# Two-layer decoder trunk on one core: the opening's loads, splits, squares and angle tables rearranged

## The reference, cut to what matters

```python
def rms_norm(x, g):
    xf = x.astype(jnp.float32)
    y = xf * lax.rsqrt(jnp.mean(xf * xf, axis=-1, keepdims=True) + RMS_EPS)
    return (y * g.astype(jnp.float32)).astype(x.dtype)

def rope_tables(positions, dim):
    inv_freq = ROPE_THETA ** (-jnp.arange(0, dim, 2, dtype=jnp.float32) / dim)
    ang = positions.astype(jnp.float32)[..., None] * inv_freq
    return jnp.cos(ang), jnp.sin(ang)

z = rms_norm(x, norm_g) @ w_in          # x: 1024 positions x 1024 channels
```

## Time and profile before

| | us |
|---|---|
| median of 3 runs | 2283.16 |
| the runs | 2282.97 to 2283.17 |
| the profiled execution's own time | 2282.51 |
| its span in the profile | 2280.4 |
| TensorE busy in the span | 2262.1 |
| start of the sum over `ssum` on TensorE | 31.23 |

### The profile page before, as it was taken

The page is one execution under the profiler, slowest core; times in us unless marked ns, Lnnn a source line. Parts: engine busy times, 40 slices in busy tenths (PEclk is TensorE's granted clock), DMA queues, the critical chain, the costliest instruction groups (busy, mean ns, idle before and its releaser), DMA issues.

```text
span 2280.4 us, 27214 instructions
## 1 busy us (share of the span) xinstructions
PE 2262.1 (99%) x10747; PEld 1869.2 (82%) x10747; DVE 1198.3 (53%) x1175; ACT 572.2 (25%) x888; POOL 881.8 (39%) x395
## 2 busy tenths in 40 slices
PE   9999999999999999999999999999999999999999
PEld 7677778888888888888888898888888888888887
DVE  7766774454555555455644244443545555554553
ACT  6455442211111111111343433422111111111110
POOL 1222217534443444334543333275334433443341
PEclk9999999999999999999999999999999999999999
DMA  5111112111111111111321021031111111111111
GB/s 196 54 47 47 33 66 80 46 50 47 46 50 52 46 46 46 55 46 51 111 84 56 27 67 63 14 138 46 56 47 46 46 55 46 46 46 54 47 47 74
DMA packets 38577, 132.29 MB, mean 58 GB/s; under 512 B 4896, under 2 KB 6752, under 8 KB 38496
## 3 DMA queue, kind: packets, MB, share of 16 engines
q1 hardware_dynamic: 35760, 122.24, 16.9%
q10 hardware_dynamic: 2736, 8.91, 1.0%
HBM read 118.26 MB, written 8.68 MB: 56 GB/s over the span
## 4 chain that ended last, share of the span: by engine, by line
PE 94%; DVE 4%; ACT 1%; issue 1%; DMA 0%; SPq 0%; DVEq 0%; ACTq 0%
PE pj L1362 42%; PE dn L1382 17%; PE pj L347 14%; PE pj L325 5%; PE pj L1826 3%; PE dn L1430 3%; PE dn L686 1%; PE pj L710 1%; PE pj L1430 1%; PE pj L506 1%; PE pj L696 1%; PE dn L1964 1%; PE dn L1973 1%; PE dn L1852 1%; PE pj L1852 1%
## 5 line engine op out<-in xcount | busy, mean ns | idle before, releaser
L1627 POOL TENSOR_TENSOR w_hi<-w_raw,ones 128x1024 fp32r<-128x1024 f32 x186 | 355.8, 1913 | 1336.9 <-PE pj L1362 564.0
L1629 POOL TENSOR_TENSOR w_lo<-w_raw,w_hi 128x1024 fp32r<-128x1024 f32 x186 | 468.2, 2517 | 14.5
L1471 DVE SCALAR_TENSOR_TENSOR ffn_y<-ffn_h,params,ffn_y 128x1024 f32<-128x1024 f32 x176 | 323.5, 1838 | 117.6 <-ACT ffn_y L1479 109.1
L1479 ACT ACTIVATE ffn_y<-ffn_h,params 128x1024 f32<-128x1024 f32 x88 | 109.6, 1245 | 886.6 <-DVE ffn_h L1460 886.6
L1460 DVE TENSOR_TENSOR ffn_h<-pj,rms_bc 128x1024 f32<-128x1024 f32 x88 | 107.8, 1224 | 365.6 <-PE pj L1362 351.9
L1520 DVE TENSOR_TENSOR res<-dn,res 128x1024 f32<-128x1024 f32 x144 | 176.1, 1223 | 115.4 <-PE dn L1382 115.4
L1362 PE MATMUL pj<-xb_hi,w_hi 128*128 128x512 f32 x704 | 216.9, 389 | 0.0
L1362 PE MATMUL pj<-xa_hi,w_hi 128*128 128x512 f32 x704 | 216.9, 389 | 0.0
L1362 PE MATMUL pj<-xb_lo,w_hi 128*128 128x512 f32 x704 | 216.7, 389 | 0.0
L1362 PE MATMUL pj<-xa_hi,w_lo 128*128 128x512 f32 x704 | 216.7, 389 | 0.0
L1362 PE MATMUL pj<-xa_lo,w_hi 128*128 128x512 f32 x704 | 216.7, 389 | 0.0
(11 more groups left out here) (314 smaller groups left out, 3555.0 us busy)
## 6 DMA issues: line engine op xcount, KB each, us to landing
w_raw<-weights SPq DMA_DIRECT2D x189, 512.0 KB, 3.5
x_first<-x_t SPq DMA_DIRECT2D x8, 512.0 KB, 8.7
res<-x_t SPq DMA_DIRECT2D x8, 512.0 KB, 7.4
scratch<-res ACTq DMA_DIRECT2D x8, 512.0 KB, 2.6
res<-scratch SPq DMA_DIRECT2D x8, 512.0 KB, 7.3
y_t<-res ACTq DMA_DIRECT2D x8, 512.0 KB, 2.6
q_turned<-q_raw SPq DMA_DIRECT2D x16, 128.0 KB, 2.3
k_turned<-k_raw SPq DMA_DIRECT2D x16, 128.0 KB, 2.3
```

The costliest lines, as they stand in the source:

```text
L1471: dve.scalar_tensor_tensor(y[:, :], h[:, SH - lag:SH - lag + S], f.tap(j, m, q), y[:, :], ALU.mult, ALU.add).then_inc(taps[f.l], 1)
L1479: act.activation(f.y[m][:, :], f.h[m][:, SH:SH + S], ACT.Identity, bias=f.tap(j, m, 3), scale=f.tap(j, m, 2)).then_inc(center[f.l], 1)
L1627: pool.tensor_tensor(whi[:, w, :], raw[:, r, :], ones[:, 0:1].to_broadcast([P, D]), ALU.mult).then_inc(w_high, 1)
L1629: pool.tensor_tensor(wlo[:, w, :], raw[:, r, :], whi[:, w, :].bitcast(F32), ALU.subtract).then_inc(w_ready, 1)
```

## The change

- Weight tiles 0 and 1 are each loaded and split in two pieces: the first 384 columns (`FIRST`, what chunks 0 to 2 need), then the other 640. TensorE waits for the first piece at chunk 0, and for the rest at chunk 3. The second warm-up uses 384 columns. Tile 2 is split as before, but stands elsewhere in the lists.
- The squares of layer 0's first norm alternate between two buffers, so that a square waits for the sum two before it.
- Positions and inverse frequencies are loaded after chunk 4. The angle instructions on ScalarE stand after the square of chunk 2, and the sines and cosines stand after the square of chunk 4, before the high part of chunk 7.
- The reduction of the angles is GpSimd's: eleven instructions on 256 columns where VectorE had eight. GpSimd's first weight split waits for the last sum of squares.

```diff
+FIRST = 3 * P
@@ pe_group
-            if first:
+            if n in (0, 1):
+                if first:
+                    pe.wait_ge(first_ready, n + 1)
+                if k * P == FIRST:
+                    pe.wait_ge(w_ready, n + 1)
+            elif first:
                 pe.wait_ge(w_ready, n + 1)
                 pe_take(pe, j)
@@ act_norm_square
-                if c > 1:
-                    act.wait_ge(norm_acc[ph], c - 1)
-                act.activation(sqt[:, :], src, ACT.Square).then_inc(norm_sq[ph], 1)
+                ahead = 2 if ph == 0 else 1
+                if c > ahead:
+                    act.wait_ge(norm_acc[ph], c - ahead)
+                act.activation(squares_of(ph, c)[:, :], src, ACT.Square).then_inc(norm_sq[ph], 1)
@@ act_mixer0
+            def sines():
+                act.wait_ge(angle_in, 1)
+                act.activation(redc[:, :], red[:, :], ACT.Abs).then_inc(red_abs, 1)
+                act.activation(sinq[:, :], red[:, :], ACT.Sin).then_inc(tabs, 1)
+                act.wait_ge(red_abs, 1)
+                act.activation(cosq[:, :], redc[:, :], ACT.Sin, bias=halfpi[:, 0:1], scale=-1.0).then_inc(tabs, 1)
             for c in range(3):
                 high(c)
             act_first_cut(act, 1)
+            act_rest_cut(act, 0)
+            high(3)
+            act_rest_cut(act, 1)
             square(0)
-            for c in range(3, KC):
+            square(1)
+            for c in range(4, KC):
                 high(c)
                 square(c - 2)
+                if c == 4:
+                    angles()
+                if c == 6:
+                    sines()
+            act_rest_cut(act, 2, 0)
             square(KC - 2)
-            act_first_cut(act, 2)
             square(KC - 1)
...
+        def pool_turns_off(pool):
+            pool.wait_ge(turn_in, 2)
+            for q, c in enumerate((c1, c2, c3)):
+                pool.tensor_scalar(turn[:, :], turni[:, :], c, None, ALU.mult).then_inc(pool_chain, 1)
+                pool.wait_ge(pool_chain, 2 * q + 1)
+                pool.tensor_tensor(ang[:, :], ang[:, :], turn[:, :], ALU.subtract).then_inc(pool_chain, 1)
+                pool.wait_ge(pool_chain, 2 * q + 2)
@@ block.gpsimd
             pool.wait_ge(set_dve, 4)
-            pool.wait_ge(w_ready, 3)
+            pool_turns_off(pool)
+            pool_fold(pool, ALU.is_gt, math.pi, -2 * math.pi, 6)
+            pool_fold(pool, ALU.is_lt, -math.pi, 2 * math.pi, 8)
+            pool_reduced(pool)
+            pool.wait_ge(norm_acc[0], KC - 1)
```

More of the change, by code:

```diff
@@ L147, in program @@
         posi = at("pos_int", [P, SQ], I32, r_b + 8 * K4)
[L148 to L154, removed]
+        ang = at("angle", [P, SQ], F32, r_b + 8 * K4 + 1024)
+        turn = at("turns", [P, SQ], F32, r_b + 8 * K4 + 2048)
+        turni = at("turns_int", [P, SQ], I32, r_b + 8 * K4 + 3072)
+        red = at("angle_reduced", [P, SQ], F32, r_b + 9 * K4)
+        redc = at("angle_size", [P, SQ], F32, r_b + 9 * K4 + 1024)
+        sinq = at("sin_packed", [P, SQ], F32, r_b + 9 * K4 + 2048)
+        cosq = at("cos_packed", [P, SQ], F32, r_b + 9 * K4 + 3072)
+        sq2 = at("sq_second", [P, S], F32, r_b + 10 * K4)
         gq8 = small("q_gain_scaled", 1)
@@ L392, in act_norm_high, with squares_of @@
             act.activation(X[0][:, c, :], src, ACT.Copy, scale=pc(PC_NORM + ph * KC + c)).then_inc(xt_hi[ph], 1)
+        def squares_of(ph, c):
+            return sq2 if ph == 0 and c % 2 == 0 else sqt
         def act_norm_square(act, ph, c, src):
@@ L411, in add_squares @@
                 eng.wait_ge(norm_acc[ph], c - 1)
-            eng.tensor_tensor(ssum[:, :], ssum[:, :], sqt[:, :], ALU.add).then_inc(norm_acc[ph], 1)
+            eng.tensor_tensor(ssum[:, :], ssum[:, :], squares_of(ph, c)[:, :], ALU.add).then_inc(norm_acc[ph], 1)
         qk_sq = sem("qk_sq")
@@ L434, in program @@
         tab_in = sem("tab_in")
+        first_in = [sem(f"first_in{n}") for n in range(2)]
+        first_high = sem("first_high")
+        first_ready = sem("first_ready")
+        pool_chain = sem("pool_chain")
         angle_in = sem("angle_in")
@@ L1091, in dve_turns_off, with pool_fold, pool_reduced @@
             c3 = two_pi - c1 - c2
[L1092 to L1101, removed]
+            pool.wait_ge(turn_in, 2)
[4 more added lines that the diff above has]
+                pool.wait_ge(pool_chain, 2 * q + 2)
+        def pool_fold(pool, cmp, edge, by, done):
+            pool.tensor_scalar(turn[:, :], ang[:, :], edge, by, cmp, ALU.mult).then_inc(pool_chain, 1)
+            pool.wait_ge(pool_chain, done + 1)
+            pool.tensor_tensor(ang[:, :], ang[:, :], turn[:, :], ALU.add).then_inc(pool_chain, 1)
+            pool.wait_ge(pool_chain, done + 2)
+        def pool_reduced(pool):
             lim = float(np.nextafter(np.float32(math.pi), np.float32(0)))
-            dve.tensor_scalar(red[:, :], ang[:, :], lim, -lim, ALU.min, ALU.max).then_inc(angle_in, 1)
+            pool.tensor_scalar(red[:, :], ang[:, :], lim, -lim, ALU.min, ALU.max).then_inc(angle_in, 1)
         def dve_lambda_sums(dve):
@@ L1148, in dve_mixer0 @@
             dve_first_cut(dve, 1)
[L1149 removed]
+            dve_rest_cut(dve, 0)
+            dve_norm(dve, 0, 3, XA, xin[:, 3, :])
+            dve_rest_cut(dve, 1)
+            add_squares(dve, 0, 1)
+            for c in range(4, KC):
                 dve_norm(dve, 0, c, XA, xin[:, c, :])
                 add_squares(dve, 0, c - 2)
[L1152 removed]
+            dve_rest_cut(dve, 2, 0)
             add_squares(dve, 0, KC - 2)
[L1154 to L1156 removed]
             add_squares(dve, 0, KC - 1)
[L1158 removed]
             dve_stat(dve, 0)
@@ L2440, in _ @@
                 sp.dma_start(xin[:, c, :], x_in[c, :, :]).then_inc(s_xin[c], 16)
-            sp_load(sp, 1, 1)
-            for c in range(3, KC):
+            sp_first_load(sp, 1)
+            sp_rest_load(sp, 0)
+            sp.dma_start(xin[:, 3, :], x_in[3, :, :]).then_inc(s_xin[3], 16)
+            sp_rest_load(sp, 1)
+            sp.dma_start(xin[:, 4, :], x_in[4, :, :]).then_inc(s_xin[4], 16)
+            sp.dma_start(posi[:, :], pos_in).then_inc(s_pos, 16)
+            sp.dma_start(invc[:, :], invf).then_inc(s_inv, 16)
+            for c in range(5, KC):
                 sp.dma_start(xin[:, c, :], x_in[c, :, :]).then_inc(s_xin[c], 16)
```

47 lines of the change are left out of this document (26 added, 21 removed).

## The result

The changed kernel took 2293.68 us in the median of five runs (2292.80 to 2294.15), the kernel before 2283.16 (2282.97 to 2283.17): 10.5 us more, a ratio of 1.0046 with the interval 1.0035 to 1.0058. The profiled execution took 2294.15 us with a span of 2292.4, so 11.6 more than before, with 12.0 more in the span (the profiled execution lay 0.65 us under its median before, and 0.47 over it after). The forecast was 2292.3, slower.

A forecast was written before the change was run, and what follows sets the result against it. TensorE, busy 99% of the span, was taken as the bound, so only the opening's sum start counted: +7.9 us for the stall and +1.2 for the clock, +9.1 on 2283.16, gave 2292.3 us, range 2286.5 to 2296.5.

The forecast's parts named there:

- One instant carries it: Opening: whatever the start of the sum over `ssum`, 31.23 us before, gains or loses goes one to one into the time.
- The earlier start: Opening: smaller first pieces start tile 1 at about 11.6 us, not 13.18, a gain of 1.5 us mostly eaten by slips.
- The sines between the chunks: ScalarE waits for GpSimd's angle until 29.6 us with chunk 7's high part queued behind; the sum starts at 39.1, +7.9 us.
- The alternation: Opening: five GpSimd instructions get in while VectorE works off its five, until about 25.6 us; the other six run free.
- Its signs: Timeline: first five GpSimd rows last 1.5 us or more, last six 0.5 to 0.7, low parts beside them over 1.5.
- GpSimd's instruction with one input: Angle reduction on 256 columns: each of six such instructions takes 0.5 us, between 0.3 and 0.7.
- The clock: TensorE after the idle stretch in the opening: slower matmuls as its clock falls, +1.2 us, thought likelier than not.
- The low part of chunk 7: Opening, behind the late high part: it comes about 0.35 us after TensorE wants it.
- The stall without the fall: Rival: TensorE waits for chunk 7 but its clock does not fall, 2291.1 us, chance 0.20.
- VectorE always wins the port: Rival: GpSimd begins in earnest when VectorE runs dry at about 24, angle at 31.3 us; 2294.0 us, chance 0.06.
- The small instructions don't shut each other out: Rival: GpSimd's 7.3 us run from 17.7 to 25.0, the sum starts at 34.5, +3.2 us; 2286.4 us, chance 0.16.
- Not slower: Rival: no shutting out, GpSimd's eleven need under 4 us, TensorE never idles for chunk 7; 2283.2 us, chance 0.06.

The follow-up runs named there:

- the kernel that keeps the clock: The changed kernel with 38 matmuls whose result nobody reads, put on TensorE ahead of the group of tile 0 and chunk 7: 2292.05 us.
- the short adds: The changed kernel with the sums of squares of chunks 2, 3 and 4 taken on one column alone: 2291.69 us.

## Why the prediction was right

**One instant carries it.** Right, by the table above: what the sum's start loses goes one to one into the time. The exception is the kernel with the sines last: there the sines, which start from no result of TensorE's, end behind the sum and hold up ScalarE's next work.

**The earlier start.** Right in size: tile 1 at 11.87 us against 11.6 in the forecast, and the turns done at 18.23 against 17.7. That it would be eaten is shown by the kernel with the pieces alone, which starts tile 1 earlier by 0.9 us and gains nothing that can be told. There it is the last add that eats it; in the changed kernel slips of 1.4 us eat it, forecast at 0.9 (at chunk 4 they were 0.9 instead of 0.6, at chunk 5 none).

**The sines between the chunks.** The step that decided, and right: ScalarE waited 9.04 us for GpSimd with chunk 7 behind it (forecast: from 21.6 to 29.6), and TensorE 9.09. Moving the sines gave back 6.3 us in the median, moving the reduction 7.6, and with neither on GpSimd's chain nor ahead of chunk 7 nothing was left, so each of the two edits needs the other to cost this much. The alternation was right as well: the five contended instructions took from 18.41 to the sixth's start at 26.07, 7.7 us, where the forecast had 17.7 to 25.6. Its signs came only in part: two of the five lasted 1.5 us or more, not all, and it was VectorE's adds that grew beyond 1.5 us, while its low parts took 1.28 and 1.41.

**The terms that were mis-sized.** The sum starts 3.0 us later than the 40.3 forecast, and three numbers make that up:
- *GpSimd's instruction with one input.* I took 0.5 us, between 0.3 and 0.7. The limit takes 0.40, but the compare with a multiplication takes 1.08, outside my bounds, and the multiplication from integers 0.86. These two lengths are above the 0.85 us that the prediction had named as a sign of being wrong, though the six free ones average 0.79. Two compares in the free part are 1.15 us more. The two-input estimate, 0.7, was right (0.72). With the turns done 0.5 us later this puts the angle at 31.22 instead of 29.6: +1.6. The nearest row I used was a two-input split of 1024 columns, and a quarter of it says nothing about what a compare costs. The Trainium skill in the GPSIMD Engine Reference (section Engine selection) says of GpSimd that with one input it is roughly at line rate. The trace doesn't agree for this operation, 1.08 against 0.28 on VectorE. By the prediction's estimate from that page's figure for two inputs, 0.81, the forecast would have been nearer in sum, but for the wrong reason: these rows are 0.72.
- *The clock.* I took 1.2 us from the warm-up's small matmuls. It was 2.9 for 14 matmuls at 0.43 instead of 0.23: +1.7. The warm-up row gave the price of one slow stretch of 128-column matmuls, not how many of TensorE's next matmuls run at the lower level. The loss net of what it hides, 2.3 us, is shown by the kernel that keeps the clock.
- *The low part of chunk 7*, 0.35 us, was hidden by the slow matmuls: -0.3.

The medians moved less than the profiled executions, 10.5 against 11.6 us. The forecast of 2292.3 is therefore 1.4 us under the median but 2.5 under what the trace shows. Part of its nearness is scatter between executions.

**The rivals.** *The stall without the fall* is out, by the clock's rows and the fillers. *VectorE always wins the port*: its time, 2294.0, is nearer to the median than mine, but its mechanism is out, since GpSimd's first instruction starts at 18.41 and five get in by 26. *The small instructions don't shut each other out* is out by 0.86 against 1.70 for the same instruction. *Not slower* asked for 0.36 us an instruction; only the last of the eleven comes near.

**What was wrong in the expectations behind it** has the same root as the clock's term: I held a wait of 2 to 3 us to be safe for the clock, and it was not.

## What to carry to other kernels

Ahead of an instruction that waits for a long chain, look at what stands behind it in its engine's queue: here a few short instructions for the sines cost 12 us in the trace, because the high part of one chunk stood behind them. Before a chain of small dependent instructions is given to an idle GpSimd, price it by its own operations and beside VectorE's two-input work: eleven took 12.8 us where VectorE's block of eight took 3.2 (21.74 to 24.98 in the kernel with the reduction there). And price an idle stretch of TensorE by the wait and the slow matmuls behind it; a start made earlier is worth only as much as the later of the two chains that meet gains.

## What the runs showed of the hardware that I had not expected

- On 128x256 GpSimd takes 0.72 us for an add of two tensors, 0.86 for a multiplication of integers by a constant, 0.40 for a limit from two sides, and 1.08 for a compare with a multiplication, which VectorE does in 0.28.
- TensorE's clock can fall in waits much shorter than the one forecast: the column read 0.50 over three us behind a wait of 2.14, and behind one of 2.46 the pairs of matmuls stood 0.85 us apart, as they did behind 9.09. It did not fall in the 1.7 us of the earlier trace rows, where the column reads 1.00 on both sides. The length of the wait alone doesn't decide: the column began to fall some 5 us into the idle time of the changed kernel (0.88 in the stretch from 30 to 31 us), but some 2 us into that of the short adds (0.90 from 28 to 29, idle from 26.76), and in four of ten executions with the sines last it probably did not fall at all. What sets how much work then runs at the lower level isn't settled by these runs. The slow matmuls at the very start are not in the column, so whether the clock is their cause is open: it reads 1.00 while the first 20 matmuls of the changed kernel come at 4.64 / 20 = 0.23 us, against 0.126 for the same form later.
- The shutting out reaches instructions of a single column beside GpSimd's short ones too, as the earlier trace rows had it beside a long one: 0.35 and 0.69 us for an add of 0.15.
